# Two layers of blocks with FFNs in Strassen form: T2 formed on VectorE in the full gate blocks, and two reorderings

## What is computed

```
def swiglu(h, w_gate, w_up, w_down):
    return (jax.nn.silu(h @ w_gate) * (h @ w_up)) @ w_down

for layer in range(2):
    x = x + 0.5 * swiglu(rmsnorm(x, norm_ffn1[layer]), ffn1_gate[layer], ffn1_up[layer], ffn1_down[layer])
    x = x + hybrid_mixer(rmsnorm(x, norm_mix[layer]), ...)
    x = x + 0.5 * swiglu(rmsnorm(x, norm_ffn2[layer]), ffn2_gate[layer], ffn2_up[layer], ffn2_down[layer])
```

## Time and profile before

| what | value |
|---|---|
| median of 3 runs | 3647.27 us (3645.16 to 3652.2) |
| the profiled execution | 3649.27 us, span 3647.4 us |
| PE / PEld busy | 3543.2 us (97%) / 3028.1 us (83%) |
| DVE / ACT busy | 2513.1 us (69%) / 1804.8 us (49%) |
| POOL busy | 285.7 us (8%) |
| DMA moved | 475.18 MB |

### The profile page before, as it was taken

One profiled execution on the slowest core, in us unless ns is written; L12 is line 12 of the kernel. 1 busy time (PEld: TensorE's weight loads), 2 busy tenths in 40 slices (PEclk: granted clock), 3 DMA queues, 4 the chain that ended last, 5 costly groups with the idle time before them and its releaser, 6 DMA issues.

```text
span 3647.4 us, 53611 instructions
## 1 busy us (share of the span) xinstructions
PE 3543.2 (97%) x20848; PEld 3028.1 (83%) x20848; DVE 2513.1 (69%) x3210; ACT 1804.8 (49%) x2527; POOL 285.7 (8%) x317
## 2 busy tenths in 40 slices
PE   9999899999999999999999999999999999999999
PEld 7776688888678887989977798999998977789988
DVE  4455666666755767787767577887888676578885
ACT  3335344436633444655555456555655554546554
POOL 0001000000200000100000220000000000310000
PEclk9999999999999999999999999999999999999999
DMA  4000256422005663577621016776777421017774
GB/s 185 36 35 35 92 162 183 140 105 93 24 35 173 173 174 117 172 199 221 176 87 57 12 53 172 201 217 179 204 204 194 133 106 50 2 63 210 207 197 132
DMA packets 70668, 475.18 MB, mean 130 GB/s; under 512 B 7952, under 2 KB 8336, under 8 KB 17552
## 3 DMA queue, kind: packets, MB, share of 16 engines
q1 hardware_dynamic: 46224, 303.97, 23.0%
q0 software_dynamic: 24192, 167.78, 21.0%
HBM read 404.62 MB, written 2.10 MB: 112 GB/s over the span
## 4 chain that ended last, share of the span: by engine, by line
PE 75%; DVE 16%; ACT 5%; DMA 2%; issue 2%; DVEq 0%; POOL 0%; ACTq 0%; SPq 0%; POOLq 0%
PE ps L670 73%; DVE split L2531 6%; ACT arena L1479 3%; DVE arena L2531 3%; PE ps L679 2%; DVE X L2535 2%; ACT split L1479 2%; DMA ring<-in_wts 2%; DVE arena L2535 2%; ACT L1479 1%; DVE arena L3629 0%; DVE ring L2531 0%; DVE small L2547 0%; DVE arena L2527 0%; DVE arena L2559 0%
## 5 line engine op out<-in xcount | busy, mean ns | idle before, releaser
L670 PE MATMUL ps<-split 128*128 128x512 f32 (+1 forms) x16236 | 2955.3, 341 | 51.2 <-DVE arena L2531 14.1
L670 PEld LDWEIGHTS ps<-split 128*128 128x128 f32 x16236 | 2506.9, 191 | 419.3 <-issue 60.3
L2531 DVE TENSOR_TENSOR split<-ring,split 128x1024 fp32r<-128x1024 f32 x674 | 823.0, 1221 | 422.7 <-ACT split L1479 372.6
L1479 ACT ACTIVATE split<-ring 128x1024 fp32r<-128x1024 f32 x674 | 709.7, 1053 | 720.9 <-PE ps L670 660.4
L1479 ACT ACTIVATE arena<-ps 128x512 f32<-128x512 f32 (+5 forms) x656 | 343.0, 523 | 377.1 <-PE ps L670 258.3
L670 PE MATMUL ps<-arena 128*128 128x128 f32 (+9 forms) x3344 | 485.5, 297 | 23.2 <-ACT arena L1479 8.8
L670 PEld LDWEIGHTS ps<-arena 128*128 128x128 f32 (+2 forms) x3344 | 393.8, 190 | 98.0 <-issue 65.6
L1479 ACT ACTIVATE split<-arena 128x1024 fp32r<-128x1024 f32 (+2 forms) x242 | 251.8, 1040 | 211.6 <-PE ps L670 131.4
L2531 DVE TENSOR_TENSOR split<-arena,split 128x1024 fp32r<-128x1024 f32 (+2 forms) x242 | 290.2, 1199 | 79.6 <-ACT split L1479 60.1
L2531 DVE TENSOR_TENSOR arena<-arena 128x512 f32<-128x512 f32 (+7 forms) x302 | 215.2, 713 | 32.7 <-ACT arena L1479 15.7
L2535 DVE SCALAR_TENSOR_TENSOR X<-ps,X 128x512 f32<-128x512 f32 x252 | 174.4, 692 | 69.0 <-PE ps L670 47.5
(11 more groups left out here) (114 smaller groups left out, 1214.2 us busy)
## 6 DMA issues: line engine op xcount, KB each, us to landing
ring<-in_wts SPq DMA_DIRECT2D x260, 1024.0 KB, 5.4
arena<-in_wts POOLq DMA_DIRECT2D x80, 1024.0 KB, 8.4
ring<-ring POOLq DMA_DIRECT2D x28, 1024.0 KB, 9.5
ring<-arena POOLq DMA_DIRECT2D x24, 1024.0 KB, 7.7
ring<-in_wts SPq DMA_DIRECT2D x41, 512.0 KB, 3.5
ring<-in_wts POOLq DMA_DIRECT2D x14, 1024.0 KB, 8.0
arena<-arena POOLq DMA_DIRECT2D x6, 1024.0 KB, 10.3
arena<-in_wts POOLq DMA_DIRECT2D x8, 512.0 KB, 4.5
```

Source lines behind the costliest of these rows:

```text
L670: return e.matmul(out, l, r, start=start, stop=stop, skip_group_check=True)
L1479: o.sig(a.activation(out, i, f, **kw), sig)
L2531: o.sig(v.tensor_tensor(out, a, b, op), sig)
```

## The change

T2 = T1 + b22 is formed on VectorE in two halves (`second`, semaphore `f_two`), from b12's slot and b22's into b11's, in all gate blocks of full width (`adds`); the half gate blocks and the down blocks keep POOL's DMA. In the first block of an FFN the halves stand in round 2, around F6's split (and a21's sum), with `two` behind them; in gate blocks followed by a down block behind N3's splits (round 2); in the others behind N5's splits (round 1). b12's and b22's loads are marked `added` with `f_two`. POOL no longer issues T2 in these blocks, nor `opened` ahead of an FFN; T4 waits for `f_two`. In the first block F5's split comes ahead of the sum for F6, N5's second split ahead of F3's sum, N3's first split ahead of F3's, and ScalarE's order is changed likewise. In down blocks N5's second split comes ahead of F6's.

```diff
@@ -243,7 +243,7 @@
 def plan():
 
     lins, loads, turned, forms, n = {}, [], [], [], 0
-    sums, shapes, before, blocks, summed_up, done, holds = 0, 0, None, 0, 0, 0, {}
+    sums, shapes, before, blocks, summed_up, seconds, downs, done, holds = 0, 0, None, 0, 0, 0, 0, 0, {}
     slots, held, kept = [0, 1, 2, 3], {}, {}
 
     def load(name, key, k0, nk, c0, ncol):
@@ -371,7 +371,7 @@
     mlp(1)
 
     def ffn(l, n_):
-        nonlocal n, blocks, summed_up, shapes, done
+        nonlocal n, blocks, summed_up, seconds, downs, shapes, done
         key, new, us = f"fgu{n_}_{l}", [], []
         old = [(len(turned) % 3, turned[-3] + 1), ((len(turned) + 1) % 3, turned[-2] + 1), ((len(turned) + 2) % 3, turned[-1] + 1)]
         if n_ == 2:
@@ -403,7 +403,7 @@
             return pc
 
         def block(name, key, p, h, kbase, c1, c2, w, at=None):
-            nonlocal blocks, summed_up
+            nonlocal blocks, summed_up, seconds, downs
             blocks += 1
             B = lins[name] = Block(name, h, p, w, at, 16 * blocks)
             B.begin, B.before = n, us[-1] if us else None
@@ -423,8 +423,16 @@
             for pc in B.of[2]:
                 summed_up += 1
                 pc.sum = ("f_t1", summed_up)
+            B.adds = B.gated and w == 512
+            downs += 16 * (not B.adds)
+            for pc in next(of for (what, _, _), of in zip(B.order, B.of) if what == "P6"):
+                seconds += B.adds
+                pc.sum = ("f_two", seconds) if B.adds else ("f_t2", downs)
+            B.two = pc.sum
             for q, b, added in (("b11", "t2", "f_t4"), ("b12", "t1", None), ("b22", "b22", None), ("b21", "t4", None)):
                 B.loads[q].end, B.loads[q].added = ("lo", end[b]), added and (added, B.count)
+            if B.adds:
+                B.loads["b12"].added = B.loads["b22"].added = B.two
             return B
 
         def down(B, a, b):
@@ -2155,7 +2163,6 @@
             if U.done:
                 a.wait_ge(S["u"], U.done)
             early(U, "P1", lambda t: F.part[:, 2 * t:2 * t + 2, :], 1.0)
-            next(extra)
             split(next(below))
             next(extra)
             split(next(below))
@@ -2176,6 +2183,8 @@
                     early(U, "P6", lambda t: at(U, t, 0), -1.0)
                 if wide and r == 5:
                     gated(U, 0, 0)
+                if U.first and r > 2:
+                    next(extra, None)
                 for y, _ in enumerate(() if U.first and r == 2 else U.of[r]):
                     split(next(below))
                     if wide and r == 5 and y == 0:
@@ -2755,6 +2764,14 @@
         for p in U.of[2][q:q + 1]:
             c = slice(p.q * U.w, (p.q + p.c) * U.w)
             tt(r["b12"][:, c], r["b12"][:, c], r["b11"][:, c], ALU.add, "f_t1")
+
+    def second(U, q):
+
+        r = {b: K.RING[:, ld.slot, :] for b, ld in U.loads.items()}
+        v.wait_ge(S[f"ring{U.loads['b22'].slot}"], U.loads["b22"].landed)
+        p = U.of[2][q]
+        c = slice(p.q * U.w, (p.q + p.c) * U.w)
+        tt(r["b11"][:, c], r["b12"][:, c], r["b22"][:, c], ALU.add, "f_two")
 
     def ln_join(name, key, splits):
 
@@ -3349,8 +3366,9 @@
                 for j in (0, 1):
                     v.wait_ge(*emptied(own_, j, g))
                 if g == 0:
+                    lo("f5", F.shape, 1)
                     tt(F.sixth, F.shape, F.a11, ALU.subtract, "h_sum")
-                    lo("f5", F.shape, 1)
+            yield
             tt(F.a12, F.sixth, F.a12, ALU.add, "h_sum")
             yield
             lo("f3", F.a12, 2)
@@ -3425,8 +3443,8 @@
             split(next(below))
             next(extra)
             split(next(below))
+            next(extra)
             split(next(below))
-            next(extra)
 
         def gate_up(U, D, late):
 
@@ -3438,8 +3456,14 @@
                 elif r == 0:
                     next(late)
                     next(late)
+                if U.first and r == 2:
+                    second(U, 0)
+                    next(extra)
+                    second(U, 1)
                 if r == 2:
                     two(U)
+                if U.first and r > 3:
+                    next(extra, None)
                 if r == 5:
                     opened(U)
                     if wide:
@@ -3458,6 +3482,8 @@
                     if r + y == 0 and not U.before.gated:
                         next(late)
                         next(late)
+                    if U.adds and not U.first and r == (2 if D else 1):
+                        second(U, y)
                     if D and r == 4:
                         added_up(after, y)
                     if r == 6 and y == 0:
@@ -3490,10 +3516,10 @@
             form(f5)
             split(next(below))
             read(U, "P1")
+            split(next(below))
             form(f6)
             split(next(below))
             tt(q["a12"], q["sum"], q["a12"], ALU.add, "shape")
-            split(next(below))
             split(next(below))
             form(f3)
             read(U, "N5")
@@ -3882,40 +3908,24 @@
     Y, M = K.y, K.m
 
 
-    F, begun = K.f, 0
-
-    def opened(U):
-
-        nonlocal begun
-        begun += 16
-        g.wait_ge(S["lo"], U.split["b11"])
-        g.wait_ge(S["f_t1"], U.of[2][-1].sum[1])
-        ld = U.loads["b11"]
-        g.dma_start(K.RING[:, ld.slot, 0:U.h * U.w], W["wts"][U.loads["b12"].i], accum_op=ALU.add).then_inc(S["f_two"], 16)
+    F = K.f
 
     def block(U):
 
         n, at = U.h * U.w, {q: K.RING[:, ld.slot, 0:U.h * U.w] for q, ld in U.loads.items()}
         b12, b22 = (W["wts"][U.loads[q].i] for q in ("b12", "b22"))
         t3 = (F.t3first if U.first else F.t3)[:, 0:n]
-        if U.first:
-            g.wait_ge(S["f_two"], begun)
-            g.dma_start(at["b11"], b22, accum_op=ALU.add).then_inc(S["f_t2"], 16)
-            g.wait_ge(S["used"], U.begin)
-            g.dma_start(t3, b22).then_inc(S["f_base"], 16)
-            g.wait_ge(S["f_base"], U.count)
-            g.dma_start(t3, b12, accum_op=ALU.add).then_inc(S["f_t3"], 16)
-        else:
-            g.wait_ge(S["lo"], U.before.split["t3"])
-            g.dma_start(t3, b22).then_inc(S["f_base"], 16)
-            g.wait_ge(S["f_base"], U.count)
-            g.dma_start(t3, b12, accum_op=ALU.add).then_inc(S["f_t3"], 16)
+        g.wait_ge(*((S["used"], U.begin) if U.first else (S["lo"], U.before.split["t3"])))
+        g.dma_start(t3, b22).then_inc(S["f_base"], 16)
+        g.wait_ge(S["f_base"], U.count)
+        g.dma_start(t3, b12, accum_op=ALU.add).then_inc(S["f_t3"], 16)
+        if not U.adds:
             g.wait_ge(S["lo"], U.split["b11"])
             g.wait_ge(S["f_t1"], U.of[2][-1].sum[1])
             g.wait_ge(S["f_t3"], U.count)
             g.dma_start(at["b11"], t3, accum_op=ALU.add).then_inc(S["f_t2"], 16)
         g.wait_ge(S["lo"], U.split["b21"])
-        g.wait_ge(S["f_t2"], U.count)
+        g.wait_ge(S[U.two[0]], U.two[1])
         g.dma_start(at["b21"], at["b11"], accum_op=ALU.add).then_inc(S["f_t4"], 16)
 
     def unit(name, begun=None):
@@ -4014,11 +4024,7 @@
         g.tensor_scalar(r1[:, j:j + 1], r1[:, j:j + 1], 1.0 / 1024, r0[:, j:j + 1], ALU.mult, ALU.add).then_inc(S["fx_m"], 1)
         g.wait_ge(S["fx_m"], j + 1)
         g.tensor_tensor(r1[:, j:j + 1], r1[:, j:j + 1], E.power, ALU.pow).then_inc(S["fx_r"], 1)
-        if j == 1:
-            opened(lins["ffn10"][0])
     for l in range(2):
-        if l:
-            opened(lins["ffn11"][0])
         for U in lins[f"ffn1{l}"]:
             block(U)
         g.wait_ge(*K.turn[f"hx{l}", 3, 1].full)
@@ -4058,7 +4064,6 @@
         first(3)
         for t in range(2, 24):
             lower(t)
-        opened(lins[f"ffn2{l}"][0])
         for U in lins[f"ffn2{l}"]:
             block(U)
 
```

## The result

The changed kernel takes 3730.37 us (median of 4 runs, 3725.2 to 3734.42) against 3648.87 for the kernel before on the same chip (4 runs, 3645.16 to 3652.2): a ratio of 1.022 [1.0201, 1.0238], 81.5 us slower. The forecast was 3720.

What follows compares the result with a forecast made beforehand. TensorE was taken as the bound, matmuls filling 97% of the span. Terms 55.7 + 10.3 + 10 - 4.2 = +71.8 us on a median of 3647.3 gave 3719, stated as 3720, 2.0% slower; range 3680 to 3750.

Steps and rivals of the forecast that it cites:

- D gates: Gate blocks followed by a down block (1 and 3 of each FFN, eight in all): net +55.7 us, clock +10.3.
- first blocks: First block of each FFN: N3 begins about 1.4 us earlier, but P6 stalls some 3 us; together +10 us, bounds -6 to +18.
- down blocks: N5's second split, moved ahead of F6's, closes a TensorE gap of 0.84 us in five blocks: -4.2 us.
- The wait in D gates: Burst of b11, b12 and T4 takes 13.6 us; VectorE waits 8.7 us for b12 ahead of the down block's T1 sum.
- TensorE 0.4 us less: In D gates TensorE stalls 0.4 us less than VectorE waits: 8.3 us, eight times 66.4.
- The clock, +10.3: Half-speed clock after each D gate stall costs half the stretch, mean 2.07 us: +10.3 us in all (0 to +17).
- Rivals A and B: D gates' burst: A shorter, 10.8 us, about +40, chance 0.17; B longer, 16.5 us, slow clock twice, +104, chance 0.09.
- Rival C: Not slower: the D gates' burst lands inside VectorE's slack, 6.6 us for 3 MB; 3637 to 3647 us, chance 0.04.
- Rival D: Change doesn't act as its text says, for instance other load slots; D gates stay: 3643 to 3653 us, chance 0.04.
- Blocks 2 and 4, 0: The two added sums behind N5's splits fit VectorE's idle time, at least 5.7 us: costed at nothing, otherwise 21 us.

Runs made afterwards that it cites:

- e1: Changed kernel with T2's halves one round earlier (round 1, behind N5's splits) in gate blocks followed by a down block: 3679.37 us, 1.0083.
- e2: Changed kernel with T2 back on POOL's DMA, without hold on b12's and b22's slots, in gate blocks followed by a down block: 3663.9 us, 1.0036.
- e5: Kernel before plus two idle VectorE operations behind N3's splits in each gate block followed by a down block, no wait on them: 3652.51 us, 1.0002.
- e6: As e5, but the next loads into b12's and b22's slots also wait for the idle operations: 3671.61 us, 1.0048 against the kernel before.
- e11: Changed kernel; in gate blocks followed by a down block T4's DMA also waits until the down block's b12 has landed: 3712.99 us, 1.0179.
- e12: Kernel before with the first blocks' new order, T2 on POOL, and two idle VectorE operations at the places of T2's halves: 3662.03 us, 1.0037.
- e3: Kernel before with only the down blocks' new order, N5's second split ahead of F6's: 3649.98 us, 1.0005.
- e14: Kernel before; in gate blocks followed by a down block T4's DMA waits until the down block's b12 has landed: 3642.29 us, 0.9975.

## Why the prediction was right, and which of its terms weren't

Three terms missed, each by more than the sum of the FFNs does; that this sum is right to 5 us is luck, since they cancel: D gates with their clock +66.0 forecast, +53.3 measured; first blocks +10, +20.7; down blocks -4.2, +3.1. The FFNs together: +71.8 forecast, +77.1 measured. With the stage that nothing touches at +8.9, the profiled execution came out 3734.4 against 3721. What was not luck is the main mechanism, the wait in D gates.

- **The wait in D gates: right in mechanism and size.** Forecast was b12 landing 13.6 us after T2's end and a wait of 8.7 us; measured 13.5 and 8.33. e1 and e2 show that nearly all of the loss depends on when T2 ends in these blocks; e5 excludes VectorE's work; e6 and e11 split it into held slots (3.4 us of wait) and T4 in the same burst.
- **"TensorE 0.4 us less": not so.** N4 does follow the T1 sum after 8.77 us with a long wait as with a short one. But VectorE comes to the sum 0.3 us later than the step had it, since the two halves of T2 delay it by 0.4 us and not by 0.1. So the wait is that much shorter, and TensorE loses all of it: 8.42 us for a wait of 8.32 in the block shown.
- **The clock, +10.3: wrong.** The step took half of each stretch at 0.50 as lost in addition to the stall. The two do not add up: P7's second half takes 5.32 us, most of it at 0.50, instead of 2.88, but N4 waits in any case for VectorE, 8.77 us after the sum. The slow clock eats idle time there, 0.84 us of gap are left, and behind those the clock is 1.00. Per gate: 5.14 + 2.44 + 0.84 = 8.42, which is what this block takes over an unstalled D gate (49.03 - 40.61). Over the eight the excess is 69.9 us, where the forecast had 82.9 (66.4 and 16.5 for the clock). Only in one of them, gate block 3 of the third FFN, is N4 slow too, for 1.4 us. e11's one gap per gate is followed by 0.50 in N4, where no gap of TensorE covers it.
- **Rivals A and B: out.** The burst was neither 10.8 nor 16.5 us. B had the two stops of TensorE right; its price for the clock fails for the same reason.
- **Rival C: out.** The fastest pair of loads in any run, e11's, took 7.2 us for 2 MB (1568.7 to 1569.1 + 6.8), 290 GB/s; 3 MB with T4 among them took 13.5 us, 233 GB/s. By the Trainium skill's 435 GB/s ("DMA: Bandwidth & Descriptors", section "Where 436 GB/s comes from") the burst would be 7.2 us as an estimate; no run came near it.
- **Rival D: out.** Loads b11 and b12 leave 0.5 us apart at T2's end, as they should if the slots are those named.
- **First blocks, +10: right place, wrong size, beyond its bound of +18.** The loss has three terms, in sum over the four FFNs. P6 starts 2.1, 0.7, 3.1 and 1.7 us later, 7.6 in all, where the forecast had 5.2 (2.2, 0.4, 2.2, 0.4); in the third N3 comes no earlier, though 1.4 us were counted on in each. The slow clock behind the gap was priced at 4.8 and took 6.6: the gap itself was forecast well (3.22 in the profile), but the same gap was followed by 0.0, 2.4, 1.4 and 2.4 us of slow clock in P6's first piece. And N4, 6.4 us, wasn't priced at all: in a first block, too, T4 now leaves with two loads; in the first FFN it left at 1530.7, took 14.2 us, and N4's first piece took 7.84 us instead of 3.45. e12, without the real T2, has none of that last term. It also varies: 6.3 us in e11 and 7.3 in e1, but 2.0 in e2, whose first blocks run the same program.
- **Down blocks, -4.2: wrong.** The step "F6 is then late, but its product begins half a product later" is true, and it stopped one product short: VectorE has no idle time between N5's second split and N3's first, so the gap reappears two products on, 0.90 us instead of 0.84 (e3). That makes the term 0; the +3.1 has another source. Before, five down blocks had the gap and took 39.6 us; the three behind a D gate with a slow N4 had none and took 38.2 to 38.4. After, one is left of the three. In all fourteen traces the 29 down blocks behind an N4 of over 7 us (6.07 in an unstalled D gate) take 38.11 to 38.80 us and the 83 others 39.57 us or more.
- **Blocks 2 and 4, 0: right**, 40.31 us in every trace, 40.41 at the most.
- **The stage before the first FFN, +8.9 in the profile, wasn't in the sum.** It is no effect of the change: see the last section.

## What to carry to other kernels

A sum moved from a DMA to a compute engine was free where it stood in idle time, but its end was also the release of two buffers and of one more DMA; cost the release before the arithmetic. When several transfers come to be released by one event, treat them as one burst of all their bytes, and ask when its last byte is needed; conversely, holding back the transfer that isn't needed soon can free the one that is (e14, 0.25%). Before pricing a reordering at the gap that it closes, follow the bound engine to its next idle time: if it has none before the next product, the gap only moves. What a stall or a slow stretch costs is read at the next wait that ends late, not at the stall.

## What the runs showed of the hardware that was not expected

**The same instructions take 1494.95 to 1503.86 us from one execution to another**, in the stretch up to the first FFN, over fourteen traces; what differs is how long TensorE ran at its lower clock, mostly early on. By the clock records it was at 0.50 for 13.7 us of this stretch in the shortest and for 30.7 us in the longest; half of the difference is 8.5 of the 8.9 us, and the other traces lie between in nearly the same order. The windows from 60 to 220 us, before and then after:

```profile
60.00:220.00 160.00, 156.20 (x818) 0.99 0.13 49
```

```profile
60.00:220.00 160.00, 156.33 (x793) 0.96 0.14 51
```

0.96 instead of 0.99 is 3% of 160 us, 5 us, with nearly the same DMA traffic (the last column, GB/s). A difference of 9 us between two profiled executions can thus lie wholly in work that is the same; stages have to be compared one by one, and small verdicts left to the timed rounds.

**A stretch at 1.2 GHz need not cost its half.** Between two gaps that one chain of VectorE sets, the clock of 0.50 lengthened a half product by 2.44 us without moving what followed. The Trainium skill ("TensorE: Matmul & The Clock Gate", section "HAM oscillation — how this bites in real kernels") puts the cost at half of the throttled time; within N4 that agrees with the stretches of the earlier trace rows, where N4 took 2.4, 1.4 and 1.4 us more than in an unstalled D gate, and not with these eight. Even behind the earlier trace rows the following down blocks took 1.2 to 1.4 us less than the others and so gave half or more of it back; I take it that VectorE's splits get ahead while TensorE is slow, which no run here shows by itself.

**An SBUF-to-SBUF accumulation is a costly neighbour, and a slow one.** T4's kind of DMA took 12.6 us at the median for 1 MB in after, where it leaves with two loads, 9.5 before and 8.2 in e14 (the pages' group ring<-ring); in D gates alone T4 took 13.1 to 14.3 us in after and 6.9 to 7.6 in e14, where it leaves behind the loads. With T4 in flight the later of the two loads landed 12.5 to 13.7 us after its issue, without it (e11) 6.7 to 8.2. Whether a plain load in T4's place would cost as much wasn't tried.
